# A four-layer hybrid block on one core: 64-row products of two head halves issued in turn, and two compressing networks issued side by side

## The reference, cut to what matters

```
# GLA (4 heads of 64): chunks with decay; scores of a pair of positions, per head
scores = einsum('bhtk,bhsk,bhtsk->bhts', qi, ki, decay)
# RWKV-7 (4 heads of 64), per position:
state = state * w_t + sa[..., None] * b_t + v_t[..., None] * k_t      # sa = state @ a_t
y = einsum('bhvk,bhk->bhv', state, r_t)
# NSA: 15 overlapping blocks of 32 tokens, 2 groups of 64 features, keys and values alike
blocks = concat(t_s[:, j:j+nc] for j in range(2)) + pos_emb
flat = blocks.reshape(B, nc, G, 32 * 64)
k_cmp = gelu(flat_k @ wk1) @ wk2        # wk1: 2048 x 256
v_cmp = gelu(flat_v @ wv1) @ wv2        # wv1: 2048 x 256
```

## Time and profile before

| | |
|---|---|
| time, median of 3 runs (lowest, highest) | 1526.08 us (1523.21, 1526.76) |
| the profiled execution: its own time, its span | 1527.97 us, 1526.7 us |
| TensorE busy, matmuls / weight loads | 1494.0 us (98%) / 1234.6 us (81%) |
| VectorE, ScalarE, GpSimd busy | 689.1, 777.3, 959.1 us |
| mean granted TensorE clock | 0.992 |
| HBM read | 225.58 MB, 148 GB/s over the span |

### The profile page before, as it was taken

How to read it: one execution, slowest core, us unless ns; L and a number is a source line. 1 busy time by engine, 2 the same in 40 slices (tenths; PEclk the granted TensorE clock), 3 DMA queues, 4 the chain that set the end, 5 groups by cost and what they waited for, 6 DMA issues and landing times. The chain is left out here.

```text
span 1526.7 us, 20723 instructions
## 1 busy us (share of the span) xinstructions
PE 1494.0 (98%) x7896; PEld 1234.6 (81%) x7896; DVE 689.1 (45%) x1088; ACT 777.3 (51%) x1230; POOL 959.1 (63%) x416
## 2 busy tenths in 40 slices
PE   7999999999999999999999999999999999999997
PEld 6988788878887888788788778888788798788886
DVE  3132865472227762645665751120337666711112
ACT  5544666445445665357443544443476345444442
POOL 6887538888885468877200278878774002498795
PEclk9999999999999999999998999999999999999999
DMA  7666325555764347564412157655553311366462
GB/s 244 181 186 179 111 84 171 174 178 161 205 175 131 98 126 231 180 192 141 132 56 56 56 154 231 180 164 197 155 169 113 111 56 56 111 181 191 140 218 97
DMA packets 121633, 227.97 MB, mean 149 GB/s; under 512 B 10304, under 2 KB 26176, under 8 KB 121536
## 3 DMA queue, kind: packets, MB, share of 16 engines
q1 hardware_dynamic: 120384, 222.46, 48.2%
q10 hardware_dynamic: 1152, 4.19, 1.0%
HBM read 225.58 MB, written 1.05 MB: 148 GB/s over the span
## 5 line engine op out<-in xcount | busy, mean ns | idle before, releaser
L179 POOL TENSOR_TENSOR parts<-raw,parts 128x1024 fp32r<-128x1024 f32 (+5 forms) x412 | 958.9, 2343 | 551.4 <-ACT parts L172 550.0
L210 PE MATMUL ps<-parts,xT 128*128 128x512 f32 (+4 forms) x2624 | 807.9, 385 | 4.4 <-POOL parts L179 0.8
L172 ACT CAST parts<-raw 128x1024 fp32r<-128x1024 f32 (+5 forms) x412 | 415.8, 1012 | 407.5 <-PE ps L210 386.7
L210 PEld LDWEIGHTS ps<-parts,xT 128*128 128x128 f32 x2624 | 487.1, 188 | 105.9 <-issue 3.7
L210 PE MATMUL ps<-parts,x_low 128*128 128x512 f32 (+3 forms) x672 | 251.5, 383 | 0.0
L210 PE MATMUL ps<-parts,M_low 128*128 128x512 f32 (+2 forms) x640 | 244.3, 386 | 0.0
L210 PEld LDWEIGHTS ps<-parts,x_low 128*128 128x128 f32 x672 | 126.6, 189 | 23.6 <-DVE x_low L2223 0.8
L210 PEld LDWEIGHTS ps<-parts,M_low 128*128 128x128 f32 x640 | 120.4, 188 | 20.4
L210 PE MATMUL ps<-parts,aT 128*128 128x512 f32 x352 | 109.5, 395 | 0.0
L210 PE MATMUL ps<-parts,H_low 128*128 128x512 f32 x272 | 106.0, 394 | 0.0
L210 PEld LDWEIGHTS ps<-parts,aT 128*128 128x128 f32 x352 | 66.0, 187 | 15.6
(11 more groups left out here) (354 smaller groups left out, 1792.2 us busy)
## 6 DMA issues: line engine op xcount, KB each, us to landing
raw<-in_w_in SPq DMA_DIRECT2D x160, 512.0 KB, 3.6
raw<-in_ffn_w_down SPq DMA_DIRECT2D x44, 512.0 KB, 4.5
raw<-in_ffn_w_gate SPq DMA_DIRECT2D x40, 512.0 KB, 3.8
raw<-in_ffn_w_up SPq DMA_DIRECT2D x40, 512.0 KB, 3.7
raw<-in_w_out SPq DMA_DIRECT2D x32, 512.0 KB, 3.5
raw<-in_w_branch SPq DMA_DIRECT2D x24, 512.0 KB, 3.4
raw<-in_w_mem_kv SPq DMA_DIRECT2D x16, 512.0 KB, 3.4
raw<-in_w_in SPq DMA_DIRECT2D x16, 366.0 KB, 3.2
```

The lines of the kernel that those rows point to most:

```text
L172: self.nc.scalar.copy(self.part(i, 0)[:, 0:nk, 0:w], self.raw(i)[:, 0:nk, 0:w]).then_inc(self.hi_ready.sem, 1)
L179: self.nc.gpsimd.tensor_tensor(self.part(i, 1)[:, 0:nk, 0:w], self.raw(i)[:, 0:nk, 0:w], self.part(i, 0)[:, 0:nk, 0:w], ALU.subtract).then ...
L210: ins = pe.matmul(b[:, 0:w], a(k0 + 2 * n + c, t), self.part(i, lo_w)[:, c, 0:w], start=(opens and n == p == 0), stop=(final and p == len( ...
```

## The change

`units` now makes both halves in one call: it takes both banks up front (`fill_two`), and issues the fp32 products in turn, rows 0 to 63 and rows 64 to 127. `compress(i)` now issues step i of the keys and then step i of the values. The keys' sums go to partitions 0 to 31 and the values' to 32 to 63, of the same 256 columns of bank 0; the blocks are padded from 30 to 32 columns with zeros, which DVE writes once a layer. The items are loaded in turn, keys and values. The 16 double steps stand in three places instead of four: X 0 comes ahead of them, then steps 0 to 6, turn_back(1) and across(1), steps 7 to 11, inverse(1), steps 12 to 15. The gelu between the two products of a network now takes 64 partitions by 256 in place of 30 by 512, and its transposes are two and not four.

```
+    def fill_two(self, pe, *uses):
+        for k, use in enumerate(uses):
+            self.index.setdefault((self.layer, use), self.filled.n + k)
+        return [self.fill_ahead(pe, use, k) for k, use in enumerate(uses)]
...
+CW = 32
...
         if s[0] == "cmp":
-            src = [(lambda n=("nsa_wk1_2", "nsa_wv1_2")[s[1]], i=i:
-                    A[n][l, :, 4 * i:4 * i + 4, :].rearrange("p (c i) f -> p c (i f)", c=2), 2, HALF) for i in range(4)]
-            parts.append((s, src, s if s[1] else None))
+            src = [(lambda n=n, i=i: A[n][l, :, 4 * i:4 * i + 4, :].rearrange("p (c i) f -> p c (i f)", c=2), 2, HALF)
+                   for i in range(4) for n in ("nsa_wk1_2", "nsa_wv1_2")]
+            parts.append((s, src, s))
...
-                def units(use, par, X, R, ring=XB):
-                    b = ring.fill(pe, (use, par))
-                    r = slice(64 * par, 64 * par + 64)
+                def units(use, X, R, ring=XB):
+                    banks = ring.fill_two(pe, (use, 0), (use, 1))
                     for n in range(4):
                         c, t = n // 2, n % 2
-                        ins = pe.matmul(b[:, n, :], X[r, c, t * P:(t + 1) * P], R[r, c, t * P:(t + 1) * P], start=True, stop=True)
-                    ring.full(ins)
+                        for par in range(2):
+                            r = slice(64 * par, 64 * par + 64)
+                            ins = pe.matmul(banks[par][:, n, :], X[r, c, t * P:(t + 1) * P], R[r, c, t * P:(t + 1) * P],
+                                            start=True, stop=True)
+                            if n == 3:
+                                ring.full(ins)
...
-                def compress(kv, i):
-                    item = W.begin(("cmp", kv)) + i // 4
...
+                def compress(i):
                     if i == 0:
...
+                    for kv in range(2):
+                        item = W.begin(("cmp", 1)) + 2 * (i // 4) + kv
+                        if i % 4 == 0:
+                            W.wait_landed(pe, item)
+                        slot = W.raw(item).rearrange("p c (i f) -> p (c i) f", i=2)
+                        ins = pe.matmul(ob[CW * kv:CW * kv + CW, 0:S], BLK[kv][:, i, :], slot[:, i % 4, :], start=(i == 0), stop=(i == 15))
...
                 pe.wait_ge(*E("k_tilde").at(1))
-                units("AK", 0, Kf, KK)
-                units("AK", 1, Kf, KK)
-                for i in range(8):
-                    compress(0, i)
+                units("AK", Kf, KK)
                 for par in range(2):
                     XB.taken(pe, ("BA", par))
                     turn_four(("X", 0), par, LA)
-                for i in range(8, 16):
-                    compress(0, i)
+                for i in range(7):
+                    compress(i)
                 turn_back(1)
                 across(1)
-                for i in range(8):
-                    compress(1, i)
+                for i in range(7, 12):
+                    compress(i)
                 inverse(1)
-                for i in range(8, 16):
-                    compress(1, i)
+                for i in range(12, 16):
+                    compress(i)
                 turn_back(2)
...
+                lane.done(v.memset(H[:, :, 0:16 * CW].rearrange("p t (i n) -> p t i n", i=16)[:, :, :, 2 * NC:CW], 0.0))
                 blocks(0, "kc")
```

More of the change, by code:

```diff
@@ L1063 @@
 FCOLS = [(j * HALF, min(HALF, FFN - j * HALF)) for j in range(6)]
-STEPS2 = ([("in", j) for j in range(7)] + [("cmp", kv) for kv in range(2)]
+STEPS2 = ([("in", j) for j in range(7)] + [("cmp", 1)]
           + [(k, j) for k in ("out_nsa", "out_mix") for j in range(2)]
@@ L1097, in second_plan @@
         shared["in", j] = (NB_, ("in", j), 0, True, True)
-    for j in range(2):
-        shared["cmp", j] = (CB, ("cmp", j), 0, True, True)
-    W.add(L, parts, lambda s: shared.get(s, (PJ, s, 0, True, True)), plain=[("cmp", 0), ("cmp", 1)])
+    shared["cmp", 1] = (CB, ("cmp", 1), 0, True, True)
+    W.add(L, parts, lambda s: shared.get(s, (PJ, s, 0, True, True)), plain=[("cmp", 1)])
 def second_layers(ctx, nc, chip, A, out, W, PJ, TP, NB_, CB, XB, GB, ST, YB, BO, OB, DB, layers=DEPTH):
@@ L1133, in second_layers @@
         BAt = H[:, :, 0:HALF]
-        BLK = [H[:, kv, 0:32 * NC].rearrange("p (i n) -> p i n", i=16) for kv in range(2)]
+        BLK = [H[:, kv, 0:16 * CW].rearrange("p (i n) -> p i n", i=16) for kv in range(2)]
         NS = H[:, :, HALF:2 * HALF]
@@ L1235, in second_layers @@
           VV = spare[1][:, 0:1024].rearrange("p (u n) -> p u n", u=8)
-          gl = [spare[1][0:2 * NC, 1024 + 512 * n:1536 + 512 * n] for n in range(2)]
+          gl = [spare[1][0:2 * CW, 1024 + 512 * n:1280 + 512 * n] for n in range(2)]
           pc = spare[2][:, 0:256].rearrange("p (t h n) -> p t h n", t=NT, h=8)
@@ L1404, in in_step_6 @@
                         pe.wait_ge(*E("tilde").at(1))
-                        units("BA", 0, KK, BP)
-                        units("BA", 1, KK, BP)
-                def compress(kv, i):
-                    item = W.begin(("cmp", kv)) + i // 4
+                        units("BA", KK, BP)
+                def compress(i):
                     if i == 0:
[L1411 to L1422, removed]
+                        CB.fill(pe, ("cmp", 1))
+                        PJ.drained(pe, (("in", 6), 1))
+                        TP.taken(pe, ("vc",))
+                    for kv in range(2):
[4 more added lines that the diff above has]
+                        ins = pe.matmul(ob[CW * kv:CW * kv + CW, 0:S], BLK[kv][:, i, :], slot[:, i % 4, :], start=(i == 0), stop=(i == 15))
+                        if (kv, i) == (1, 15):
+                            CB.full(ins)
+                        elif i % 4 == 3:
+                            ins.then_inc(W.used.sem, 1)
                 def compressed():
@@ L1427, in compressed @@
                     pe.wait_ge(*E("gelu").at(1))
-                    for n in range(4):
-                        ins = pe.transpose(b[:, n * 2 * NC:(n + 1) * 2 * NC], gl[1][:, n * P:(n + 1) * P], chip.ident[0:2 * NC, 0:2 * NC])
+                    for f in range(2):
+                        ins = pe.transpose(b[:, f * 2 * CW:(f + 1) * 2 * CW], gl[1][:, f * P:(f + 1) * P], chip.ident[0:2 * CW, 0:2 * CW])
                     TP.full(ins)
@@ L1522, in gla @@
                 def gla(n):
[L1523 to L1527, removed]
+                    if n:
+                        pe.wait_ge(*E("pn").at(n))
+                    units(("g", n), *((FT[:, F_GK:F_GK + 2, :], FT[:, F_GQ:F_GQ + 2, :]) if n == 0 else
+                                      (PN[:, (n - 1) % 2], PN[:, (n - 1) % 2])), ring=ring_of(n))
                 def four(use, par, X, R):
@@ L1689, in _ @@
                 pe.wait_ge(*E("r_tilde").at(1))
-                units("RB", 0, BP, Rf)
-                units("RB", 1, BP, Rf)
+                units("RB", BP, Rf)
                 inverse(2)
@@ L1706, in _ @@
                 inverse(4)
-                units("RK", 0, Kf, Rf)
-                units("RK", 1, Kf, Rf)
+                units("RK", Kf, Rf)
                 head_sums("bn", "rkr")
@@ L2395, in gelu_in @@
                 def gelu_in():
-                    b = CB.read(dve, ("cmp", 1))[0:2 * NC, :]
+                    b = CB.read(dve, ("cmp", 1))[0:2 * CW, 0:S]
                     lane.done(v.tensor_copy(gl[1], b))
@@ L2410, in compressed @@
                     lane.done(v.tensor_copy(HIDk.rearrange("p f (g m) -> p f g m", g=2)[:, :, :, 0:NC],
-                                            b[:, 0:4 * NC].rearrange("p (f g c) -> p f g c", f=2, g=2)))
+                                            b[:, 0:4 * CW].rearrange("p (f n) -> p f n", f=2)[:, :, 0:2 * NC].rearrange("p f (g c) -> p f g c", g=2)))
                     for f in range(2):
                         ins = v.tensor_copy(HIDv[:, f, :, :].rearrange("p b (g m) -> p b g m", g=2)[:, :, :, 0:NC],
-                                            b[:, (4 + 2 * f) * NC:(6 + 2 * f) * NC].rearrange("p (g c) -> p g c", g=2).unsqueeze(1)
+                                            b[:, (2 * f + 1) * CW:(2 * f + 1) * CW + 2 * NC].rearrange("p (g c) -> p g c", g=2).unsqueeze(1)
                                             .to_broadcast([P, 4, 2, NC]))
```

2 lines of the change are left out of this document (1 added, 1 removed).

## The result

The changed kernel takes 1509.42 us (median of 4 runs, 1508.34 to 1510.77), and the kernel before, beside it, 1525.27 us: a ratio of 0.9897, with a 95% interval of 0.9882 to 0.9912. Forecast were 1511 and 0.990. The profiled execution took 1510.77 us, its span is 1509.5, 17.2 less than in the earlier trace rows, and the mean granted clock is 0.992 as before. A few executions (of the kernel before and of one variant) took 1543 to 1550 us at a mean clock of 0.975 to 0.977, and the medians leave them out.

What follows compares the result with a forecast made beforehand. PE was taken as the bound, busy 1494.0 of 1526.7 us. 4.45 (units) + 3.25 (networks) = 7.7 us a layer, 15.4 in two, off the median 1526.08: 1511 us predicted, forecast 1507 to 1516 (0.58), range 1503 to 1520.5.

Steps and rivals of the forecast that it cites:

- the cover: Networks on PE: the longer steps hid DVE's mask and SP's loads; three waits come out, together 3.8 us a layer.
- Pairs of units: 64-row products: alternating halves take 1.16 us in place of 1.71 for 16 records; 4.45 us a layer saved.
- The networks: Blocks of compress: two column groups side by side save 7.1 us a layer before waits, 3.25 after them.
- X 0: Transposes ahead of the steps: the second half waits 1.6 us for DVE's mask of AK's bank.
- The loads: Ahead of steps 8 to 11 and 12 to 15, PE waits 1.3 and 0.8 to 0.9 us for items to land.
- the first wait: Ahead of steps 8 to 11: PE waits 1.3 us for the values' item to land.
- the second: Ahead of steps 12 to 15: PE waits 0.8 to 0.9 us for the second item to land.
- the rival of milder waits: AK's mask done sooner and loads overlapping more; with none of the 3.8 us of waits, 1503 us; chance 0.12.
- Small edits: Zeros on DVE cost 0.1 us, two fewer transposes bring 0.1 to 0.2, the smaller gelu brings nothing.
- Column groups taking turns: Rival in the networks' steps: 0.216 us for each record, a layer gains 3.0 us, 1520 us; chance 0.15.
- draining the array: Rival: each change of column group costs some 0.2 us, a layer loses 3.4 us, 1533 us; chance 0.05.
- The clock: Rival: new PE waits make the clock fall for some 7 us, costing up to 3.5 us a layer, 1518; chance 0.10.

Runs made afterwards that it cites:

- The one column group: Changed kernel with keys' and values' sums both in partitions 0 to 31, in two halves of the bank, copied by DVE in two pieces; 1521.75 us, ratio 0.9961.
- The networks alone: Changed kernel with a pair's row halves one after the other and each bank awaited in its turn; 1517.20 us, ratio 0.9932.
- DVE's order: Changed kernel with DVE's softmax of nsa(0) moved behind the values' blocks and the mask of AK; 1508.70 us, ratio 0.9875.
- the last version: Changed kernel with DVE's softmax behind blocks and mask, double steps 8, 4, 4, and two between the halves of X 0; 1505.59 and 1506.16 us.

## Why the prediction was right, and where its terms were off

**The time.** 15.9 us won by the medians, 15.4 forecast; 1509.42 us lies in the forecast's 1507 to 1516. The mechanism held: both kinds of tiles run side by side, and the cover comes back as waits. That the number is so close is in part luck, since a wait that was put too long and costs that were left out almost cancel.

**Pairs of units.** 4.45 us a layer were forecast. Measured in the third layer: 0.55 each for BA, AK and RK (by the record counts and lengths above, 1.16 for 1.71), 0.43 for RB and what follows it up to g 0, 0.19 for g 0, 0.21 and 0.21 for g 1 and g 2 (from g 2's first record to the transposes behind the scores it is 1.95 us, and was 2.16), nothing to speak of for g 3, and 0.55 each for the last three: 4.34. That g 0 would give 0.2 and not 0.55, because DVE's mask stands ahead of across(3), and g 3 nothing, because PE waits for DVE in increment(2), came out so; the wait there is still 0.54 us.

**The networks.** The blocks run as forecast: both groups side by side, 0.216 us for a record of each. The one column group shows that nothing else makes them short.

**X 0.** 1.6 us of wait forecast, in differences of starts; measured so, it is 1.73 (1.56 in the view of waits). The networks alone, with 1.01, and DVE's order, with 0.63, move it as the chain on DVE says.

**The loads: mis-sized.** "two of 524 KB at 255 GB/s land 2.06 us apart". They landed 1.2 us apart (3.8 and 4.6 us after their issue). 255 GB/s is the mean of three microseconds in which the loads of before overlapped only in part, and not what a pair in flight together gets: after the change 401 GB/s were moved from 756 to 757 us. So the first wait was 0.58 us and not 1.3 (1.4 by the prediction's own 758.3 and 759.7); the second, 0.84, came out at the 0.8 to 0.9 forecast. AK to turn_back(2) thus won 4.42 us, where 0.55 + 3.25 were forecast: 0.8 from the first wait, less 0.2 for X 0 and the second. Of the rival of milder waits, this part came true.

**Left out: both banks up front.** The prediction took `fill_two` for free, since in the kernel before PE waits for no bank there. In the last layer RK reaches the bank 0.44 us early, and the pair's saving is nearly gone; the 0.11 us ahead of g 0 in each layer are probably of this kind too.

**Small edits.** The zeros cost 0.11 us on DVE (0.1 forecast), the fewer transposes brought 0.1 (0.1 to 0.2), and the gelu nothing on the path.

**Rivals.** Column groups taking turns, or draining the array: refuted by 3.22 us against 6.23. The clock: 1.00 from 745 to 770. The stretch that held the clock's fall towards 1.2 GHz before has its like after: 0.83 as the mean of 815 to 845 us before and of 810 to 840 us after, and 0.992 over both executions. In the last layer the fall is deeper in the profile after (0.56 as the mean from increment(2) to g 4, 0.68 before), and that stretch takes 11.58 us, 10.62 before; but in the two repeats of the changed kernel it takes 10.61 and 10.52, so this is not the change's doing.

By segments the change gives 8.3 us in the third layer (4.34 - 0.55 of AK + 4.42 + 0.1) and 7.8 in the fourth, where RK's wait costs 0.45 (g 1 to RK 9.18 us, 8.94 before): 16.1 in two. Where the clock falls, from increment(2) to g 4, the profile after loses 1.0 us in the two layers. The profiled spans differ by 17.2; the 2.1 us that are left lie in stretches that the edit doesn't touch.

## What to carry to other kernels

Where two products use different rows or different columns of the array, issue them in turn: here this took row halves from 1.71 to 1.16 us and column groups from 6.23 to 3.22 us. Before doing so, list what the longer version covered: of the 7.0 us a layer that the networks' records lost, 3.2 came back as waits, for a mask on another engine and for slots of a weight ring that free in pairs. Those waits, not TensorE, are what to work on next, first by the order on the engine that is waited for, and move behind other work only what really waits: the half of X 0 that needn't wait was hidden already.

## What the runs showed of the hardware

Two fp32 tiles of 128 rows by 32 columns, with moving operands of their own, ran together with no loss: 0.216 us for one record or for one of each (28 records in 3.15 us to the next start, and in 6.16 in one group).

TensorE's records overtake those of the other row half only within a reach: with eight records of one half ahead, the other starts about 0.55 us late (a pair takes 1.71 us), with four ahead, 0.01 us after the first (1.26 us; 1.16 in strict turns). The reach lies somewhere between; nothing finer was measured.

A block of two column groups costs about 0.1 us to leave (3.15 us for 14 x 0.216 = 3.02), so that splitting the blocks further is cheap: the last version has one more, and its segment from AK to RB, 18.22 and 18.48 us, reached the 18.2 to 18.6 expected.
